# Dots of gathered rows: five in three gate steps throughout, and three more of them behind the gates

## What is computed

```python
q = (tokens @ w_query).reshape(Ntok, PEER_HEADS, 2, PEER_DK)
s = jnp.einsum('nhpd,hpkd->nhpk', q, sub_keys)
s_top, i_top = lax.top_k(s, K)
...
best, pos = lax.top_k(cand, K)
expert_idx = jnp.take_along_axis(cand_idx, pos, axis=-1)
gate = jax.nn.softmax(best, axis=-1)
...
u = jnp.take(expert_down, idx, axis=0)
a = jax.nn.gelu(jnp.einsum('nd,nhkd->nhk', xb, u), approximate=False)
w = (gb * a)
v = jnp.take(expert_up, idx, axis=0)
return jnp.einsum('nhk,nhkd->nd', w, v)
```

## Time and profile before

| what | us |
|---|---|
| median of three runs (1582.76 to 1584.28) | 1583.2 |
| the profiled execution, its own time | 1584.32 |
| its span, first to last instruction | 1582.4 |
| PE busy in the span | 1565.8 |
| DVE busy | 1164.6 |
| POOL busy | 963.6 |
| ACT busy | 663.3 |

### The profile page before, as it was taken

How to read it: one execution, slowest core, us unless ns; L and a number is a source line. 1 busy time by engine, 2 the same in 40 slices (tenths; PEclk the granted TensorE clock), 3 DMA queues, 4 the chain that set the end, 5 groups by cost and what they waited for, 6 DMA issues and landing times.

```text
span 1582.4 us, 26079 instructions
## 1 busy us (share of the span) xinstructions
PE 1565.8 (99%) x9937; PEld 1483.6 (94%) x9937; DVE 1164.6 (74%) x2263; ACT 663.3 (42%) x994; POOL 963.6 (61%) x555
## 2 busy tenths in 40 slices
PE   8999999999999999999999999999999999999997
PEld 6888888888989999999999999999999999999997
DVE  5155351251579999999999883338999999998995
ACT  5352452552434444444444544334334333333433
POOL 4463326523235899887778778876757665564741
PEclk9999999999999999999999999999999999999999
DMA  5232252313424999989999999879999999999981
GB/s 196 88 103 67 73 158 95 115 54 118 149 84 130 302 347 349 330 285 313 379 399 397 396 410 393 309 248 365 411 410 406 399 406 409 395 404 393 400 354 54
DMA packets 129697, 438.91 MB, mean 277 GB/s; under 512 B 13888, under 2 KB 28224, under 8 KB 121280
## 3 DMA queue, kind: packets, MB, share of 16 engines
q1 hardware_dynamic: 60592, 227.43, 39.6%
q0 software_dynamic: 46080, 167.79, 27.8%
q10 hardware_dynamic: 22928, 42.41, 7.0%
HBM read 395.21 MB, written 41.81 MB: 276 GB/s over the span
## 4 chain that ended last, share of the span: by engine, by line
PE 50%; DVE 4%; DMA 3%; issue 1%; POOL 1%; ACT 0%; ACTq 0%; POOLq 0%
PE psum L1589 16%; PE psum L1590 16%; PE psum L1591 16%; DMA arena<-down_rows,kept 3%; PE psum L1905 2%; DVE arena L1415 1%; DVE arena L1250 1%; POOL w_low L470 1%; POOL arena L502 0%; DVE arena L1410 0%; DVE arena L1411 0%; DVE arena L1323 0%; DVE kept L1375 0%; DVE arena L1383 0%; PE psum L1941 0%
## 5 line engine op out<-in xcount | busy, mean ns | idle before, releaser
L470 POOL TENSOR_TENSOR w_low<-kept,w_high 128x1024 fp32r<-128x1024 f32 x205 | 500.7, 2445 | 316.8 <-ACT w_high L603 306.1
L1589 PE MATMUL psum<-hT_high,w_high 128*128 128x352 f32 (+2 forms) x1392 | 477.6, 343 | 1.7 <-POOL w_low L470 1.7
L1591 PE MATMUL psum<-hT_high,w_low 128*128 128x352 f32 (+2 forms) x1392 | 470.6, 338 | 0.0
L1590 PE MATMUL psum<-hT_low,w_high 128*128 128x352 f32 (+2 forms) x1392 | 470.6, 338 | 0.0
L1590 PE MATMUL psum<-wgt_low,up_high 128*128 128x352 f32 x1016 | 330.0, 325 | 0.0
L1589 PE MATMUL psum<-wgt_high,up_high 128*128 128x352 f32 x1016 | 328.7, 324 | 0.0
L1591 PE MATMUL psum<-wgt_high,up_low 128*128 128x352 f32 x1016 | 327.5, 322 | 0.0
L603 ACT ACTIVATE w_high<-kept 128x1024 fp32r<-128x1024 f32 x211 | 222.6, 1056 | 129.6 <-PE psum L1591 91.2
L1589 PEld LDWEIGHTS psum<-hT_high,w_high 128*128 128x128 f32 x1392 | 262.1, 188 | 14.5 <-issue 2.9
L1590 PEld LDWEIGHTS psum<-hT_low,w_high 128*128 128x128 f32 x1392 | 262.3, 188 | 11.8 <-issue 0.5
L1591 PEld LDWEIGHTS psum<-hT_high,w_low 128*128 128x128 f32 x1392 | 262.0, 188 | 12.0
(11 more groups left out here) (285 smaller groups left out, 1957.3 us busy)
## 6 DMA issues: line engine op xcount, KB each, us to landing
kept<-down_in SPq DMA_DIRECT2D x128, 512.0 KB, 6.4
arena<-up_pairs SPq DMA_DIRECT2D x64, 1024.0 KB, 9.2
kept<-front_w SPq DMA_DIRECT2D x92, 512.0 KB, 3.5
gate_dram<-arena ACTq DMA_DIRECT2D x40, 512.0 KB, 11.0
arena<-hid_dram SPq DMA_DIRECT2D x52, 352.0 KB, 12.7
arena<-gate_dram SPq DMA_DIRECT2D x8, 1280.0 KB, 14.0
kept<-gate_dram SPq DMA_DIRECT2D x8, 1280.0 KB, 14.2
hid_dram<-arena ACTq DMA_DIRECT2D x52, 176.0 KB, 6.6
```

The source lines that it names most:

```text
L470: nc.gpsimd.tensor_tensor(lower, ring[:, p % RING, :], high.bitcast(F32), ALU.subtract).then_inc(low_ready, 1)
L1589: nc.tensor.matmul(out, lhs[0], rhs[0], start=first, stop=False)
L1590: nc.tensor.matmul(out, lhs[0], rhs[1], start=False, stop=False)
L1591: return nc.tensor.matmul(out, lhs[1], rhs[0], start=False, stop=last)
```

## The change

The two tables get other numbers. In `DOTS_STEP` the first ten steps that had two dots each and the pattern 1, 2, 2 behind them become one pattern, 2, 2, 1, from step 2 to the last; step 1, which had none, gets one. The dots in the gate steps go from 74 to 71, and those behind them from 32 to 35. In `DOTS_END`, the blocks with one gather go from 22 to 19, and from then on there are two. Nothing else differs.

```diff
-DOTS_STEP = (0, 0) + (2,) * 10 + (1, 2, 2) * 10 + (2, 2)
-DOTS_END = (1,) * 22 + (2,) * 5
+DOTS_STEP = (0, 1) + (2, 2, 1) * 14
+DOTS_END = (1,) * 19 + (2,) * 8
```

## The result

The changed kernel takes 1587.28 us in the median (1584.5 to 1589.05), the kernel before 1583.22 beside it: a ratio of 1.0023, 95% interval 1.0017 to 1.0029, so 4.1 us slower (2.7 to 4.6). That lies inside the range of the prediction, but 0.02 us from its upper end, 2.4 us above the forecast, and by the bound of 0.2% it is more likely slower than the same, which the prediction had given 0.78. The profiled execution took 1586.85 us, its span is 1584.9.

What follows compares the result with a forecast made beforehand. PE, busy 1565.8 of 1582.4 us, bounds the kernel, so only its waits for POOL's low halves can move the time. The terms -1.76 + 0.51 + 2.20 + 0.70 = +1.65 us on 1583.2 gave 1584.9 us, range 1582.0 to 1587.3.

Steps and rivals of the forecast that it cites:

- the bound of 0.2%: Whole kernel: 3.2 us, what a measurement can tell from no change; 1580.0 to 1586.4 us counts as the same.
- What bounds the kernel: PE is busy 1565.8 of 1582.4 us; reordering dots and gathers moves time only through PE's waits for POOL's low halves.
- The waits removed, -1.76: Gate steps: PE's waits before block 64 (1.29 us lost) and block 73 (0.47 us) both go.
- The wait added before block 56, +0.51: Early gate steps: the dot in step 1 delays DVE, so block 56's low half comes 0.51 us late; bounds 0 to 1.0.
- POOL's lead, +2.20 with the 0.15: Behind the gates: six pairs each take 0.94 us of POOL's 3.59 us lead; blocks 119 to 121 start 2.20 us late.
- The hold of the ring, +0.70: Pairs behind the gates: late rows in the four-slot ring hold POOL for two turns at 8.4 us; 0.70 us lost.
- The limit of 8.06 us: Pairs behind the gates: time a row may take from issue to landing before the four-slot ring holds POOL.
- Rival (b): Pairs behind the gates: pairs and weights saturate DMA, rows take 9.5 us, ring costs 2.9 us; +3.85, 1587.1 us; chance 0.20.
- The last dots hidden: Behind the gates: the last dot moves out by some 7 us at most, covered because its first user stands behind block 124.
- The sum: Whole kernel: -1.76 + 0.51 + 2.20 + 0.70 = +1.65 us, 1584.9 us in the median.
- The chance of 0.20 for slower: Whole kernel: chance given to a time slower by more than 3.2 us, beside 0.78 for the same and 0.02 for faster.
- What would make it wrong: Up products behind block 127: the forecast fails if they gain or lose time of their own; the change touches nothing there.

Runs made afterwards that it cites:

- the steps alone: The changed kernel's DOTS_STEP with the old DOTS_END, which then ends in five pairs; 1584.51 us, ratio 1.0007 to the kernel before.
- the late load: The changed kernel with the second 1 MB load of up rows issued two groups of weights later; 1585.34 us, ratio 1.0016 to the kernel before.
- the end alone: The kernel before with the new DOTS_END and the old DOTS_STEP, so four pairs behind the gates; 1586.03 us, ratio 1.0017.
- the spread pairs: The changed kernel with its six pairs behind the gates kept apart by two single gathers; 1583.06 us, ratio 0.9993 to the kernel before.

## Why the prediction was right in its path and off in two of its terms

**What bounds the kernel**: right. What the changed kernel lost in the gate steps and behind them is, in its trace, nearly all waits of PE for a low half that stands behind a gather.

**The waits removed, -1.76**: the term that was over-sized. The means of the traces with old and new steps give -0.53, and the kernel with the steps alone agrees in time: 1.0007 is +1.1 us (-0.3 to 2.5), and -0.53 + 1.25 is +0.72. Two steps of the argument failed. First, I took the waits of one execution for waits of the kernel; that execution was 1.1 us over the median, and I named the difference and drew nothing from it. Second, that POOL's pair "now needs the first dot of step 20, not both, which alone starts the low half about 1.15 us sooner" took it that the rows of the dots ahead land in time. The wait before block 64 is gone in all eight traces with the new steps, as forecast; the one before block 73 is not, 0.67 us lost in the changed kernel's trace. The chain that ended last, there (start, us, what; gathers 56 and 71):

```profile
719.18 9.11 DMA arena<-down_rows,kept
763.65 11.10 DMA arena<-down_rows,kept
```

In the three traces with a wait before block 73 the rows of gathers 71 and 72 took 10.1 to 11.1 us; in the five without, that of 72 took 8.7 to 9.2. DVE stands still for late rows, and its one-hot tiles of step 20 are 2.9 to 3.2 us ahead of PE in the three and 5.4 to 5.9 in the five. The dot in step 1 alone does not decide it: it takes DVE's lead in the early steps (forecast with the wait before block 56, and found: at step 3 the tiles are 2.94 us ahead instead of 7.38), but it stands in all eight, and by step 11 the changed kernel's lead is 6.88 us against 5.43 before. Why these rows are late in some executions is open.

**The wait added before block 56, +0.51**: its place and size were right for the profiled execution (0.61), but it stands in two of eight traces. In these the row of gather 56 took 9.1 and 9.3 us, in the other six 8.2 to 8.5: its bound of 0 for a row that lands sooner was the usual case.

**POOL's lead, +2.20 with the 0.15**: right. 2.27 us measured where nothing else disturbs it (the late load), at blocks 119, 120 and 121 as 0.39, 0.92 and 0.96; 1.25 against 1.26 with five pairs.

**The hold of the ring, +0.70**: mis-sized, and on a wrong ground. The limit of 8.06 us bears out: rows of 8.84 and 9.78 us held POOL by 0.80 and 0.94, rows of 5.3 and 7.3 did not. But I took two turns at 8.4, as if pairs and weights brought every row near the 8.29 us of the earlier trace rows, and it was one turn at up to 9.78, from one load: 1.74 us. That load stood in the trace of the kernel before, on SP's queue, and I did not reckon with it:

```profile
1023.54 0.58 SPq L378 DMA_DIRECT2D arena<-up_pairs  x1
```

The row of 8.29 us is that of gather 152, issued 0.16 us ahead of it; none of the seven rows behind, the three pairs among them, took over 7.95. Rival (b) gave the time, 1587.1, and not the mechanism; its rows of 9.5 us came in one turn, not in both, and pairs and weights alone, in the kernel with the late load, held nothing. The Trainium skill, DMA: Bandwidth & Descriptors, section Queues, rings and completion order, says that each engine takes turns between the queues that have work for it; a gather on POOL's queue and a load on SP's then share the same engines, and the rows of 8.84 and 9.78 beside the load against 5.3 and 7.3 without it agree.

**The last dots hidden**: right, with 9.4 us to spare.

**The sum.** -0.53 + 2.25 + 1.74 = +3.46 us, inside the measured 2.7 to 4.6. The other kernels close too, with intervals nearly as wide as the terms: the end alone, 0.32 + 1.64 = 1.96, measured 1.3 to 4.1 (its trace has 2.2 us won by the pace and 1.6 lost by the clock besides, both told in the last section); the late load, -0.53 + 2.27 + 0.6 = 2.3, measured 1.1 to 4.0; the spread pairs, -0.53, measured -2.5 to 0.3. The chance of 0.20 for slower was too small: both mis-sized parts, the gate steps by 0.7 us and the ring by 1.0, pointed the same way, and with both right the sum is past the bound of 3.2. That 1587.28 still lies inside a range that ends at 1587.3 is luck.

**What would make it wrong**, the last sentence of the prediction, named the up products, "which nothing in the change touches". They did change: in the changed kernel's trace they are 1.65 us shorter than before, by the change of pace and less the wait of 1.29. The sum above leaves this out: with it the sum is +1.8, under the measured 2.7, so it holds only if most timed executions lack the change or lose as much elsewhere. How many have it is open; the 20 times of the changed kernel spread over 4.55 us, those of the kernel before over 2.65.

## What to carry to other kernels

Where an engine in program order runs some blocks ahead of the one that sets the time, count its lead, what each block of the heavy kind takes from it, and what each light one gives back: six pairs in a row cost 4 us, the same six with two singles between them nothing. Before a slot of a ring is counted on, look which large transfers of other queues are issued within its turn, and before such a transfer is moved, what it will meet at the new place. A wait that hangs on the landing of a transfer should be read from several executions, and the distance of the profiled one from the median says how far to trust it.

## What the hardware showed that I had not expected

**Two paces at the same granted clock.** With the clock at 1.00 in both stretches, which is the level of 2.4 GHz, and DMA at 1.02 in both, PE's products of 352 columns start 160.0 or 161.1 ns apart on average. In the faster pace the starts are even to 1 ns; in the slower they repeat a pattern from about 158 to 165 ns. Once in a pace, the stream stays there for hundreds of products. In all traces the up products begin in the slower one. In the spread kernel the stream fell from the faster to the slower at 1047.4 us, behind one interval of 192 ns, without a wait. Behind the gates waits left it in either: with the late load it kept the faster pace behind 0.15 and 0.68 us and had the slower behind 0.70. In the up products waits of 0.67 to 2.6 us led to the faster one. What decides the direction is open, and so is what the two paces come from.

**The clock behind a standstill.** In the kernel with the end alone, the granted clock fell to half, the level of 1.2 GHz, from 1040.2 to 1043.6 us, right behind the wait of 1.79 us before block 119. The rows by stretch (columns as above):

```profile
1036.00:1040.00 4.00, 2.21 (x14) 1.95 (x14) 2.46 (x4) 1.41 (x2) 3.80 (x4) 1.00 1.03 408
1040.00:1042.00 2.00, 2.00 (x9) 2.00 (x8) 1.78 (x3) 0.00 (x0) 2.00 (x1) 0.55 0.99 342
1042.00:1044.00 2.00, 2.00 (x9) 2.00 (x9) 0.68 (x2) 0.00 (x0) 2.00 (x2) 0.59 0.37 139
```

The timeline of PE at the two ends of that stretch:

```profile
1040.11 0.40 PE L1590 MATMUL psum<-hT_low,w_high 128*128 128x352 f32 x1
...
1043.74 0.32 PE L1591 MATMUL psum<-hT_high,w_low 128*128 128x352 f32 x1
```

The 13 products from the first to the second take 3.63 us instead of 13 x 0.16 = 2.08: 1.55 us lost with no wait that any list shows. The changed kernel stood still for 1.88 us in the same place and kept its clock at 1.00, so this comes on top in some executions only; it may be part of the 0.6 us between the sum and the measured median, which no run here shows.
